# Three transposes of a chunked recurrence rearranged, and the start of two layers reordered

## The reference

```python
def rms_norm(x, g):
    y = x * rsqrt(mean(x * x, -1) + EPS) * g
def hybrid_layer(x, ...):            # twice (DEPTH = 2)
    h = rms_norm(x, norm_g); z = h @ w_in; ...
    return x + merged @ w_out
def wkv_bidir(r, k_d, v, kk, w, a, state0):      # 8 heads of 64, 2 directions
    def step(s, inp):                            # s: 64 x 64 per head and direction
        sa = einsum(s, -kk_t)
        s = s * w_t + sa * (kk_t * a_t) + v_t * k_t
        y_t = einsum(s, r_t)
# once over 256 context tokens (only the state is kept), then over 256 latent tokens
```

## Time and profile before

| | |
|---|---|
| median of 3 runs | 2692.46 us (2689.22 to 2692.95) |
| the profiled execution, its own time | 2685.37 us |
| its span, first to last instruction | 2683.5 us |
| PE busy / DVE busy / ACT busy | 2552.9 / 927.9 / 582.7 us |
| share of the chain that ended last: PE / ACT / DVE / DMA | 93% / 3% / 2% / 1% |

### The profile page before, as it was taken

How to read it: one execution, slowest core, us unless ns; L and a number is a source line. 1 busy time by engine, 2 the same in 40 slices (tenths; PEclk the granted TensorE clock), 3 DMA queues, 4 the chain that set the end, 5 groups by cost and what they waited for, 6 DMA issues and landing times.

```text
span 2683.5 us, 42917 instructions
## 1 busy us (share of the span) xinstructions
PE 2552.9 (95%) x18398; PEld 1678.9 (63%) x18398; DVE 927.9 (35%) x2019; ACT 582.7 (22%) x1166; POOL 150.0 (6%) x125
## 2 busy tenths in 40 slices
PE   7999999998999999999997788899999999999998
PEld 6866887887885887888886677433333333333333
DVE  1763363312186345322465754411111111111112
ACT  2100233300100123220234533311111111111112
POOL 0050000000023000000002321000000000000000
PEclk9999999999999999999999999999999999999999
DMA  6546232344445432326420002899999999999996
GB/s 233 209 168 212 102 126 95 126 157 159 157 167 209 165 108 103 125 95 215 170 83 3 4 4 97 369 428 428 428 429 428 428 428 428 428 428 428 428 429 254
DMA packets 135048, 636.18 MB, mean 237 GB/s; under 512 B 5136, under 2 KB 5408, under 8 KB 109152
## 3 DMA queue, kind: packets, MB, share of 16 engines
q1 hardware_dynamic: 133904, 629.78, 59.0%
q0 software_dynamic: 1008, 4.37, 0.4%
HBM read 633.08 MB, written 1.05 MB: 236 GB/s over the span
## 4 chain that ended last, share of the span: by engine, by line
PE 93%; ACT 3%; DVE 2%; issue 1%; DMA 1%; SPq 0%; ACTq 0%; DVEq 0%
PE bank L265 26%; PE bank L2550 17%; PE bank L2578 9%; PE bank L455 6%; PE bank L477 4%; PE bank L286 4%; PE bank L1332 4%; PE bank L1381 4%; PE bank L2512 2%; PE bank L2541 2%; PE bank L2498 2%; PE bank L1625 1%; PE bank L353 1%; PE bank L2570 1%; ACT hidT L2661 1%
## 5 line engine op out<-in xcount | busy, mean ns | idle before, releaser
L265 PE MATMUL bank<-hT,ring 128*128 128x256 f32 x3136 | 695.0, 382 | 12.9 <-DVE hT L706 12.9
L265 PEld LDWEIGHTS bank<-hT,ring 128*128 128x128 f32 x3136 | 596.5, 191 | 106.8 <-DVE hT L706 14.7
L2550 PE MATMUL bank<-ring,hsel 128*64 128x512 f32 x2112 | 461.8, 595 | 0.0
L2550 PEld LDWEIGHTS bank<-ring,hsel 128*64 128x64 f32 x2112 | 149.0, 137 | 310.9 <-issue 310.6
L2823 DVE TENSOR_SCALAR glu<-bank 128x256 f32<-128x256 f32 x66 | 28.0, 425 | 754.6 <-PE bank L2550 751.2
L2578 PE MATMUL bank<-ring,hidT 128*64 128x512 f32 x1024 | 226.8, 595 | 22.0 <-ACT hidT L2661 22.0
L739 DVE SCALAR_TENSOR_TENSOR a_buf<-v_pad,par,a_buf 128x256 f32<-128x256 f32 x480 | 215.8, 532 | 0.0
L2578 PEld LDWEIGHTS bank<-ring,hidT 128*64 128x64 f32 x1024 | 70.5, 137 | 156.2 <-issue 128.1
L1381 PE MATMUL bank<-ring 64*64 64x64 f32 (+1 forms) x5888 | 136.1, 225 | 28.9 <-issue 13.4
L1381 PEld LDWEIGHTS bank<-ring 64*64 64x64 f32 x5888 | 123.2, 137 | 43.6 <-issue 16.2
L2652 ACT ACTIVATE sig<-glu 128x256 f32<-128x256 f32 x66 | 27.5, 417 | 458.8 <-DVE glu L2823 458.8
(11 more groups left out here) (425 smaller groups left out, 2477.4 us busy)
## 6 DMA issues: line engine op xcount, KB each, us to landing
ring<-in_w SPq DMA_DIRECT2D x196, 2048.0 KB, 16.7
ring<-in_w_in SPq DMA_DIRECT2D x66, 2048.0 KB, 7.8
ring<-in_w_ada SPq DMA_DIRECT2D x12, 2048.0 KB, 8.0
ring<-in_w_ret_out SPq DMA_DIRECT2D x8, 2048.0 KB, 8.0
ring<-in_w_out SPq DMA_DIRECT2D x6, 2048.0 KB, 8.5
ring<-in_w_conv_out SPq DMA_DIRECT2D x4, 2048.0 KB, 8.6
ring<-in_w_attn_out SPq DMA_DIRECT2D x4, 2048.0 KB, 8.0
extra<-in_w SPq DMA_DIRECT2D x2, 2048.0 KB, 34.9
```

The lines of the kernel that those rows point to most:

```text
L265: mm = nc.tensor.matmul(out[:, j, :], w[:, k, col + j * P:col + (j + 1) * P], rhs[:, k, :], start=(k == 0), stop=(k == DC - 1))
L2550: mm = nc.tensor.matmul(half(flat[4 + b], side), g["hsel"][:, 2 * (j % 2) + k, j // 2, :], w[:, at:at + UNIT], start=False, stop=(j == 3 a ...
```

## The change

1. **Starts of layers.** `par` is held for both layers and fetched once at the program's start. `cons` is no longer among the transfers that all engines wait for (there are three now) and is issued behind the second weight unit. ScalarE loads the root's table by an unread activation, takes the root right behind the sum, and the exponential of the decays after it. `h_ready` is signalled per piece, and TensorE's first product waits piece by piece.
2. **Transposes of sB and sK (context), of sB (latents)** are joined to `pairs` and to `keys`: the right side of the matmul is 128 wide, 64 columns of sA and 64 of a unit matrix `turner` that lies in the ring buffer beside it. `by_token("sB")` goes in all turns, `by_token("sK")` in context turns; in latent turns it moves from k = 3 to k = 2. The results stand in banks 0 and 1 (6 and 7 for sK) beside the product, and ScalarE copies tB ahead of level 0 and tK at k = 1 (latents: k = 2). `t1(0)` waits for tB's copies.
3. **V** is transposed from its own buffer `m_v`; the copies sV go.
4. `first` gets banks 4 and 5 and so stands behind the wait for U's copies; `pairs` has a signal of its own (`paired`), at which VectorE starts MP. tB is kept twice, the state in another buffer.
5. New waits on `tok_out`: before `g0_state` in context turns, and in turn 2 before `lora(1, 3, 6)`.

```diff
@@ features
+                if p == 0 and j == 0:
+                    pe.wait_ge(g["h_ready"].sem, g["h_ready"].at(l, k + 1))
@@ hybrid_tensor
-    pe.wait_ge(g["h_ready"].sem, g["h_ready"].at(l, 1))
...
+        if l == 0 and u == 1:
+            pe.wait_ge(g["cons_in"].sem, g["cons_in"].at(None, 1))
@@ hybrid_scalar
+    def root_table():
+        nc.scalar.activation(g["unread"][0:1, l:l + 1], g["eps"][0:1, 0:1], ACT.Sqrt)
+    if l:
+        root_table()
...
+    if l == 0:
+        nc.scalar.activation(g["cond"][:, :, 0:2], ..., ACT.Silu).then_inc(g["cond_ready"].sem, 1)
+        root_table()
...
+    root(rows[:, 0, :], stat[0], D, "x_root")
+    act.wait_ge(g["par_in"].sem, g["par_in"].at(None, 1))
     nc.scalar.activation(g["lam"][:, :], par[:, a:a + 8], ACT.Exp).then_inc(
...
-    root(rows[:, 0, :], stat[0], D, "x_root")
@@ hybrid_pool
-    pool.dma_start(g["par"][:, :], g["par_dram"][bass.ds(l, 1), :, :].rearrange("o p n -> (o p) n")).then_inc(
@@ hybrid_loads
+        if l == 0 and n == 1:
+            sp.dma_start(g["cons"][:, :], g["cons_dram"][:, SHARED_CONST:CONST_WIDTH]).then_inc(
@@ mixer_memory
+    g["with_turner"] = lambda dc: flat[:, dc * 3 * C2:2 * DN * 3 * C2 - dc * 3 * C2].rearrange("p (k w) -> p k w", k=2)[:, :, 0:C2]
@@ mixer_tensor
-        both_ways(pairs)
-        both_ways(first, "first_done", True)
+    def pairs(turn):
+        def product(d, c):
+            dc = d * NC + c
+            out = flat[d][:, c * 2 * C2:(c + 1) * 2 * C2].rearrange("p (k w) -> p k w", k=2)
+            return halves(out, g["sB"][:, dc, :], g["with_turner"](dc), turned=d == 1)
+        pe.wait_ge(g["staged"].sem, g["staged"].at(turn, 1))
+        both_ways(product, "paired")
+    def firsts():
+        def product(d, c):
+            dc = d * NC + c
+            return halves(chunk(4 + d, c, NC * C2), g["sA"][:, dc, 0:C2], g["sB"][:, dc, :], turned=d == 1)
+        both_ways(product, "first_done", True)
...
                 if turn == 2:
+                    pe.wait_ge(g["tok_out"].sem, g["tok_out"].at(turn, 6))
                     lora(1, 3, 6)
...
-                if k < 4:
-                    both_ways(by_token(("sV", "sB", "sK")[k - 1]))
+                if k == 1:
+                    both_ways(by_token("m_v"))
+                if k == 2 and lat:
+                    both_ways(by_token("sK"))
...
+            if k == 0:
+                pe.wait_ge(g["tok_out"].sem, g["tok_out"].at(turn, 2))
             both_ways(t1(k), "t_done")
...
         if keep_state and turn != STEPS - 1:
-            front(turn + 1)
+            pairs(turn + 1)
         pe.wait_ge(g["u_out"].sem, g["u_out"].at(turn, 2))
+        if keep_state and turn != STEPS - 1:
+            firsts()
         if keep_state:
             both_ways(state_rates, "s_done")
@@ mixer_scalar, step
+        for d in range(DIRS):
+            act.wait_ge(g["pairs_out"].sem, g["pairs_out"].at(turn, d + 1))
+            nc.scalar.activation(g["tB"][turn % 2][:, d * NC:(d + 1) * NC, :], ..., ACT.Copy).then_inc(
...
+                if k == 1 and not lat:
+                    act.wait_ge(g["pairs_out"].sem, g["pairs_out"].at(turn, d + 3))
+                    nc.scalar.activation(g["tK"][:, d * NC:(d + 1) * NC, :], ..., ACT.Copy).then_inc(
@@ mixer_vector
-                v.tensor_copy(g["sV"][:, h, :], g["m_v"][:, :, s])
...
+        for d in range(DIRS):
+            dve.wait_ge(g["paired"].sem, g["paired"].at(turn, d + 1))
+            v.tensor_tensor(g["MP"][:, d * NC:(d + 1) * NC, :], flat[d].rearrange("p (n w) -> p n w", n=NC)[:, :, 0:C2],
@@ program
-            sp.dma_start(hyb["cons"][:, :], shared["cons_dram"][:, SHARED_CONST:CONST_WIDTH]).then_inc(start_in.sem, start_in.one())
+            pool.dma_start(hyb["par"][:, :, :], shared["par_dram"].rearrange("l p n -> p l n")).then_inc(
```

More of the change, by code:

```diff
@@ L183, in hybrid_memory @@
     sb("pair", [2, T])
-    sb("par", [PAR_WIDTH])
+    sb("par", [DEPTH, PAR_WIDTH])
+    sb("unread", [DEPTH])
     sb("cons", [CONST_WIDTH - SHARED_CONST])
@@ L512, in hybrid_scalar @@
 def hybrid_scalar(act, nc, g, l):
-    par = g["par"]
+    par = g["par"][:, l]
     def take(p, out, func):
@@ L524, in hybrid_scalar @@
             g["x_squared"].sem, g["x_squared"].one())
[L525 to L528, removed]
+    if l == 0:
+        nc.scalar.activation(g["cond"][:, :, 0:2], g["mpar"][:, MIX_PAR["cond"]:MIX_PAR["cond"] + 2 * DC].rearrange(
+            "p (c s) -> p c s", s=2), ACT.Silu).then_inc(g["cond_ready"].sem, 1)
+        root_table()
     def root(out, ssq, n, signal):
@@ L537, in hybrid_scalar @@
     root(rows[:, 0, :], stat[0], D, "x_root")
+    act.wait_ge(g["par_in"].sem, g["par_in"].at(None, 1))
+    a = PAR["decay"]
+    nc.scalar.activation(g["lam"][:, :], par[:, a:a + 8], ACT.Exp).then_inc(
+        g["lambda_ready"].sem, g["lambda_ready"].one())
     act.wait_ge(g["decay_sum"].sem, g["decay_sum"].at(l, 1))
@@ L688, in mod_take @@
                                 bias, ALU.add).then_inc(g["mod_part"].sem, g["mod_part"].one())
-    par, step, rows, sm = g["par"], g["dve_step"], g["rows"], g["small"]
+    par, step, rows, sm = g["par"][:, l], g["dve_step"], g["rows"], g["small"]
     stat = [g["bank"][7][:, 0, :], g["bank"][3][:, 0, :]]
@@ L1417, in step @@
         new_col = C2 * (1 + turn % 2)
+        token = [chunk_start(lat, i, d) for d in range(DIRS)]
         def by_token(name):
@@ L1422, in product @@
                     to = 64 - lo if d else lo
-                    mm = nc.tensor.matmul(chunk(d, c, NC * C2)[to:to + 64], g[name][lo:lo + 64, d * NC + c, :],
-                                          ident[lo:lo + 64, lo:lo + 64], start=True, stop=True)
+                    src = g["m_v"][lo:lo + 64, c, token[d]:token[d] + C2] if name == "m_v" else g[name][lo:lo + 64, d * NC + c, :]
+                    mm = nc.tensor.matmul(chunk(d, c, NC * C2)[to:to + 64], src, ident[lo:lo + 64, lo:lo + 64],
+                                          start=True, stop=True)
                 return mm
@@ L1532, in between @@
                 pe.wait_ge(g["state_ready"].sem, g["state_ready"].at(turn, 0))
+                if not lat:
+                    pe.wait_ge(g["tok_out"].sem, g["tok_out"].at(turn, 6))
                 both_ways(g0_state, "g0_done", True)
@@ L1602, in mixer_tensor @@
     lora(1, 1, 6)
-    front(0)
-    g["first_done"].n = 0
+    pairs(0)
+    firsts()
+    g["first_done"].n = g["paired"].n = 0
     for turn in each_turn(g, 2 * STEPS, SCAN):
@@ L1795, in keep_x0 @@
                     g["x0_out"].sem, g["x0_out"].one())
+        for d in range(DIRS):
+            act.wait_ge(g["pairs_out"].sem, g["pairs_out"].at(turn, d + 1))
+            nc.scalar.activation(g["tB"][turn % 2][:, d * NC:(d + 1) * NC, :],
+                                 flat[d].rearrange("p (n w) -> p n w", n=NC)[:, :, C2:2 * C2], ACT.Copy).then_inc(
+                g["tok_out"].sem, g["tok_out"].one())
         for k in range(LEVELS):
```

80 lines of the change are left out of this document (41 added, 39 removed).

## The result

The changed kernel takes 2661.31 us (median of 4 runs, 2658.26 to 2662.53) beside 2692.7 us for the kernel before (median of 4; one took 10795.36 us, which is a slow run and left out of the ratio, the others 2689.22 to 2692.95): ratio 0.9893, interval 0.9873 to 0.9913. That is 31 us less by the medians and 29 by the ratio (23 to 34). The two profiled executions are 24.1 us apart: 2685.37 us before, 2661.23 after, where 2659.1 was predicted for that pair and 2666 for the median.

A forecast was written before the change was run, and what follows sets the result against it. The prediction took TensorE, 93% of the chain, to bound the kernel. Layer starts 19.1 us and recurrence 7.2 us make 26.3 us less than 2692.5, so 2666 us, range 2656 to 2678.

The forecast's parts named there:

- (a): Recurrence, front of each turn: 0.2 us won per front, 1.0 in turns 0 to 4, nothing in turns 5 to 7.
- (b): Recurrence, turn 2: TensorE newly waits ahead of lora for the copies of tV and tK, 2.0 us more, once.
- (c): Recurrence, context turns: two products removed in each, 1.9 us less in all (bounds 0 and 4.1).
- (e): Recurrence, context turns: 128 records fewer per turn, half an instruction block, 3.0 us less in all (at most 7.2).
- Layer 1's start: Projection starts 8.0 us earlier after the sums, and the clock stays at its upper level, 2.8: together 10.8 us less.
- Layer 0's start: Projection starts at 18.0 instead of 24.50 us, 6.5 less, and the clock gives 1.8: together 8.3 (5.5 to 9.5).
- B: Rival, layer starts: the clock falls there all the same, 4.6 us less gain, 2671 us; chance 0.1.
- (d): Recurrence, latent turns: the product at k = 3 goes, 0.8 us less in each of four turns, 3.3 in all.
- A: Rival, recurrence: the gaps named issue don't depend on the number of instructions; gain 22.0 us, 2670 us; chance 0.2.
- C: Rival: instructions bind TensorE in the whole recurrence, which gives 11 us; all 30 us less, 2662 us; chance 0.13.
- D: Rival, recurrence: joining the transposes wins nothing, tB's copies come late every turn; recurrence 5 us slower, 2678 us; chance 0.1.
- E: Rival, recurrence: TensorE, with less to do, is granted the lower clock; 16 us slower than before, 2708 us; chance 0.02.

The follow-up runs named there:

- one_h_ready: The changed kernel, but TensorE's first product of a layer waits for all 8 pieces of hT at once: 2679.01 us, ratio to before 0.9946.
- the second execution: The changed kernel run and traced once more, unaltered: 2666.31 us, ratio to before 0.9910.
- rates_before_y: The changed kernel with the latents' copies of tB issued ahead of those of y on ScalarE: 2665.05 us, ratio to before 0.9901.
- ctx_filler: The changed kernel with two unread transposing products of V put back into each context turn, at k = 2 and 3: 2666.29 us in one execution.
- wide_split: The changed kernel with each 128 wide product in pairs and keys issued as two of 64 columns: 2675.12 us in one execution.
- scan_only: The kernel before with only the recurrence's edits: 2683.13 us, ratio to before 0.9975.
- the halves: The kernel before with only the layers' starts changed (ratio 0.9940, 17.6 us less), and with only the recurrence changed (0.9975, 6.9 us less).

## Why the prediction was right, and where it wasn't

**The sum.** 26.3 us were predicted. The profiled pair shows 24.1, the medians 31 (23 to 34), and 2661.3 lies in the range. The starts' mechanisms held and carry most of the gain. That the total of the profiled pair came within about 2 us of the forecast is in part luck: the recurrence gave 3.6 less than its 7.2, and falls of the clock that the list didn't have gave 4.9, less 1.6 for a new one. Of the recurrence's parts (a), (b) and the sum of (c) and (e) were mis-sized, and (e) by itself isn't shown.

**Layer 1's start (10.8): right.** 7.9 for 8.0 in the gap, 2.6 for 2.8 in the clock. The eight pieces, the hidden table load and the absent transfer are in the trace as costed, and `one_h_ready` shows that the clock's part hangs on the short idle time.

**Layer 0's start (8.3): 8.0 in this execution, 6.0 in the second.** The projection was to start at 18.0, with the weights at 17.7 and the root's path at 18.0; it starts at 18.12, released by the weights. The two were indeed a tie, with the other one last. The clock's term (1.8) measured 1.6 in the profiled execution and was absent in the second, as in three of nine: there B was right. In those three the sums and the `ada` unit ended at 16.4 to 16.5 us, and not at 16.8 or later, and the weights let the projection start at 18.4 to 18.5, so the gap was about 2 us instead of 1.2 to 1.4. The prediction had no row for an idle time between 1 and 9 us.

**What the list lacked.** Clock falls later in the program are part of the starts' effect. The one near 1052 us went (2.9 us), and one near 399 us came (1.6, and 2.9 in the second execution). All nine executions with the short gap have the second, and eight of them lack the first; `rates_before_y` and `one_h_ready` have both. The step "nothing behind them is tied to an absolute time" failed: it is true of the work, not of the clock.

**(a) The front (-1.0).** The win is about 0.1 per front and not 0.2: from `u` to MP it took 1.79, 1.84 and 1.69 us in turns 5 to 7, and now takes 1.61, 1.70 and 1.61; in turn 3 it is 0.13 less, in turn 1 nothing. The forecast took one turn for all. Its loss in turns 5 to 7 was predicted from a queue on ScalarE; the queue is the last wait in turn 6, but `rates_before_y` shows that without it the turns win no more than executions differ by. (The sum for tB there is 4.90 and not 4.94; nothing hangs on it.)

**(b) The wait ahead of `lora` (+2.0): measured +3.0 up to `d1`, +3.4 for the turn, 2.8 by taking it away.** The mechanism, the place and the end of the wait were right (2.67 us behind `t1(1)`; 2.57 by the prediction's 1487.4 and the earlier trace rows). `lora` was sized at 1.06 from the kernel before, but it ran at the lower clock level and took 2.0. After a standstill the work behind it is to be priced at either level: behind the same wait of 2.00 us `lora` took 2.08 us in seven executions and 1.14 in `ctx_filler`.

**(c) and (e), context (-4.9): `ctx_filler` gives -3.9, and 3.7 of it in turns 0 and 1.** Both were sums over four like turns; they were not alike. VectorE is busy for 12.7 us of turn 0 and for 16.9 to 17.9 us of the others, which fits turn 0 but not the win in turn 1. The part (e), by instruction blocks, isn't shown: fewer blocks came, 54 for 57, as predicted, but 22 waits without a releaser stayed 22 and their sum didn't leave the scatter. "The same issue waits with fewer blocks" stood among the signs of being wrong, and for the records that were taken away it came about.

**(d), latents (-3.3, with 0.2 of the front): -3.4.** The sum is right (0.8 x 4 is 3.2, as written 3.3), but it was to be 0.8 in each turn, and the turns gave 0.9, 1.6, -0.8 and 1.7. No run parts its two causes, TensorE's work and the instruction blocks.

**The rivals.** A is refuted by `wide_split` where records are added, and not where the change takes them away. B is refuted in layer 1 and true in three of nine executions in layer 0. C (instructions bind everywhere) is refuted for turns 2 and 3; but `wide_split`, +8.6 us for 3.8 blocks, 2.3 us each, lies nearer to its 3.6 than to nothing. C's own sum was 1.2 too large: 10.8 + 1.0 - 2.0 is 9.8, not 11. D is refuted by turns 0 and 1, and by `scan_only` as a whole, though its wait for tB was real in turn 6. E showed nothing: the recurrence's mean clock is 0.98 before, and 0.97 and 0.98 in the two executions of the changed kernel.

**Open:** the total's exact size. The first set of executions gave 31 us, the second 23.7, the halves 24.5 and the traces 24 to 25; the intervals overlap, and falls of the clock shift from execution to execution. The median of all nine executions of the changed kernel is 2662.53 us, which makes the gain about 28. Open too are the recurrence's share in it and which of its waits are instruction blocks.

## What to carry to other kernels

A short serial path at the start of a stage pays twice: by its own length, and by the clock that TensorE is granted behind it, so an edit that makes an idle time of 9 us one of 1 us, or brings it back to 4, is to be priced with the first unit at either level. Where small matmuls run densely, don't price their instructions at nothing: splitting the wide products in two cost 8.6 us, and TensorE's busy time grew by 1.2 of it only. But a run that adds records doesn't prove what taking some away is worth. A wait that is added "once" deserves the same look as the loop's: it took back 3.4 us, about as much as the latents won, and moving two copies ahead on ScalarE's queue, with the waits that go with them, won the turn back.

## What the hardware showed beyond expectation

**The clock falls move.** In each layer the same eight products (L412, before L408) follow the same idle time of 2.11 us. Layer 0 and layer 1, in the kernel before:

```profile
406.78 1.99 PE L408 MATMUL bank<-ak,cons 128*128 128x256 f32 x8 [2.11 <-DVE ak L843]
```

```profile
1050.87 2.96 PE L408 MATMUL bank<-ak,cons 128*128 128x256 f32 x8 [2.11 <-DVE ak L843]
```

and in the changed kernel:

```profile
398.82 3.64 PE L412 MATMUL bank<-ak,cons 128*128 128x256 f32 x8 [2.11 <-DVE ak L858]
```

```profile
1034.05 1.99 PE L412 MATMUL bank<-ak,cons 128*128 128x256 f32 x8 [2.11 <-DVE ak L858]
```

with the granted clock at 0.50, its lower level of 1.2 GHz, in the third:

```profile
398.80:402.20 3.40, 3.38 (x8) 2.52 (x8) 0.00 (x0) 0.60 (x1) 0.00 (x0) 0.50 0.00 0
```

With the start's edit hundreds of microseconds earlier, the fall moved to the other of two like places, in eight of nine executions; in `rates_before_y` both places pay (3.31 and 3.33 us). What decides it isn't shown, and whether a shift of the start alone would do it wasn't tried.

**Instruction supply.** 963 more small records for the same arithmetic cost 8.6 us in 221, while PE's busy time grew by 1.2.
